# One packed constant table for three, loaded from ScalarE's queue together with the large tile's x

## The chip, the cores and the metric

The kernel runs on one core of a Trainium2 chip. The metric is device time in microseconds for one execution of the whole step; a time of a kernel is the median of its runs.

## What is computed

The reference is one inference step of one hybrid decoder layer: 2048 prompt tokens behind 16 learned meta tokens, and 8 decoding sequences of 4 tokens, all of width 1024. One projection feeds four token mixers of width 256, each mixer is gated, and the four go together through an output projection.

```python
h = rmsnorm(x, norm_pre)
c = split(h @ w_in)                       # 14 groups of 256 columns, and 16 for the low rank
log_a = log_sigmoid(c.a_lr @ gla_w_a2 + gla_b_a) / 16
o_a = gated_linear(c.a_q / 8, c.a_k, c.a_v, log_a, s_gla)      # 4 heads of 64
o_b = c.b_b * causal_conv3(c.b_c * c.b_v) * silu(c.b_z)
o_c = gated_linear(silu(c.c_q) / 8, 1 - f, c.c_i, log f, s_hgrn)
o_d = (trailing_means(c.d_v) - c.d_v) @ pool_w * pool_scale * silu(c.d_z)
x = x + rmsnorm(concat(o_a, o_b, o_c, o_d) @ w_out, norm_post)
```

The two gated linear mixers also get a head norm and a SiLU gate. `gla_w_a2` with its bias is the gate matrix (`a2` in the kernel), `pool_w` are the pool weights (`pw`), and the masks (`cu8`) are the byte masks that VectorE uses in the running sums (keep or restart) and in copying scores.

## The kernel before

The tokens are cut into a small tile 0 (16 meta tokens and the 32 sample tokens, T0 = 48) and eight large tiles of 256 tokens, each loaded in two chunks of 128 rows. So x(1, 0) and x(1, 1) are the two halves of the first large tile. Both halves go into the same buffer `xin`, so that x(1, 1) may be loaded only when the transposes of x(1, 0) have read it.

All engines run hand-written orders. Before the steady loop the kernel prepares its weights: `w_in` comes as 28 units of 512 KB (`unit`, L411 to L418), eight staging areas lie in the buffers `wo_hi` and `wo_lo` (units 0 to 3 and 4 to 7 of each round), and each unit is turned into an fp16 upper half on ScalarE (`upper`, L1245) and an fp16 rest on VectorE (`lower`, L1827). A unit from number 8 on is loaded when `lower` has freed its staging area. Matmuls are done as three fp16 products.

The start is ordered as follows.

- SyncE (L420 to L440) issues: meta and sample tokens (L373, L374), the table `cf32` (L421), the low-rank weights (L422), x(1, 0) (L382), units 0 and 1, the gate matrix `a2` of 97 rows (L426), the masks `cu8` (L427), units 2 and 3, the pool and convolution states, then x(1, 1) behind a wait for the transposes of x(1, 0), units 4 to 7, the two recurrent states, `pw` (L437), and units 8 to 27.
- ScalarE (L1536 on): table load, low-rank weights (L1539, which needs VectorE's L2204, and that needs `cf32` and the low-rank weights), norm of tile 0, norm of x(1, 0), upper half of tile 0's activations (L1292), `upper` 0 and 1, `upper` 2, the low-rank output of tile 0 (L1303), upper half of x(1, 0) (L1292), the logarithm for tile 0, `upper` 3, norm of x(1, 1) (L1267), `upper` 4 and 5, upper half of x(1, 1), and so on.
- TensorE: transposes of tile 0 and of x(1, 0) (L762), the low rank of tile 0 (L733), the gate product (L746, needs `a2`), transposes of x(1, 1), then projections (L695).
- VectorE: its part of the norms (L1842), the rest of the activations (L1858), `lower` 0 to 2, x(1, 0), the first running sum (L1880, needs `cu8`), `lower` 3, x(1, 1) (L1842, L1858), then `lower` 4 to 7 and on.

In the profile, `cu` is the mask table, `a` the gate matrix, `cf` the table `cf32`, `X<-in_w_lr` the low-rank weights.

Of the kernel before, what the change touches and what calls it, by code (L numbers as in the profile page):

```python
# [8 lines left out]
U8 = mybir.dt.uint8  # L9
# [5 lines left out]
GW = 256  # L15
NCF, NCU = 319, 1024
HK = 64
RANK = 16
LRG = 3
LRP = 2 * RANK * LRG  # L20
# [5 lines left out]
CH = 128  # L26
# [18 lines left out]
NSTAGE = 8  # L45
# [21 lines left out]
def fill_order():  # L67
# [29 lines left out]
    xin=32, xre=32, yst=32,  # L97
# [5 lines left out]
    gs=28, ge=14, gm=28, sc=32, am=32,  # L103
# [17 lines left out]
def nth(name, i, k):  # L121

    if name in ("tcp", "tlc"):
        return 1 if i == 0 else 2
    if name in ("xhi", "xlo", "hx"):
        return (i - TURNED) * SIGNALS[name] + k
    if i == 0:
        return k
    return (0 if name in OWN0 else FIRST.get(name, SIGNALS[name])) + (i - 1) * SIGNALS[name] + k


def dims(i):

    return (T0, 1, T0) if i == 0 else (TT, 2, CH)
# [18 lines left out]
def program(nc, a, outs):  # L153
    ctx = ExitStack()
    with ctx:
        def sb(name, shape, dt=F32):
            return ctx.enter_context(nc.sbuf_tensor(name, shape, dt))
# [13 lines left out]
        XIN = sb("xin", [128, D])  # L171
# [9 lines left out]
        X1, X3, X4 = (sb(f"X{n}", [128, 2, TT + 16]) for n in (1, 3, 4))  # L181
        X2 = sb("X2", [128, 2, TT])
        cf32 = sb("cf32", [128, NCF])
        cu8 = sb("cu8", [128, NCU], U8)
        pw = sb("pw", [128, 2, 128])
        a2 = sb("a2", [LRP + 1, GW])
        lrb = sb("lrb", [LRP + 1, TT])
        cst = sb("cst", [128, 2])
        sx = sb("sx", [128, 3])
# [7 lines left out]
        ident, bones, gs = cf32[:, 0:128], cf32[:, 128:256], cf32[:, 256:256 + KD]  # L197
# [15 lines left out]
        tin = X4[:, :, :].rearrange("p j t -> p (j t)")  # L213
# [81 lines left out]
        def keys_of(i, br, rows):  # L295
# [8 lines left out]
        s0 = {n: ctx.enter_context(nc.semaphore("f_" + n)) for n in OWN0}  # L304
        s["pj"] = ctx.enter_context(nc.semaphore("s_pj"))
        once = {n: ctx.enter_context(nc.semaphore("o_" + n)) for n in (
            "cf32", "cu8", "a2", "lrw", "tin", "pw", "smp", "zero", "cst", "gs", "wlr", "wlrh", "gp",
            "whi", "wlo", "wohi", "wolo", "ylast", "lsq", "xlast", "sdec", "vx", "su", "sv", "svout", "tl", "sout", "fin", "pd0",
            "act", "dve", "pool")}
        for n in range(NSTAGE):  # L310
# [6 lines left out]
        def sem(name, i):  # L317
            return (s0 if i == 0 and name in OWN0 else s)[name]

        def at(name, i, k):  # L320
            if i == 1 and k == 0 and name in OWN0:
                i, k = 0, FIRST.get(name, SIGNALS[name])
            return sem(name, i), nth(name, i, k)
# [21 lines left out]
        def bank(i, name):  # L345
            return pj[FILL[i, name] % 2]

        block = ctx.enter_context(nc.Block())
        dve, act, pool, pe = nc.vector, nc.scalar, nc.gpsimd, nc.tensor
# [20 lines left out]
        def _(sp):  # L370
            def load_x(i, c):
                if i == 0:
                    sp.dma_start(XRES[0:META, :], a["meta_tokens"]).then_inc(sem("xin", i), 16)  # L373
                    sp.dma_start(XRES[META:T0, :], a["x_sample"].rearrange("b t d -> (b t) d")).then_inc(sem("xin", i), 16)  # L374
                    return
                if c == 0 and i > 1:
                    sp.wait_ge(*(at("xt", i - 1, 4) if i <= TURNED else at("xlo", i - 1, 2)))
                elif c == 1:
                    sp.wait_ge(*(at("xt", i, 2) if i < TURNED else at("xlo", i, 1)))
                if c == 0 and i == 2:  # L380
                    sp.wait_ge(once["su"], 4)
                sp.dma_start(XIN[:, :], a["x_prompt"][(i - 1) * TT + c * CH:(i - 1) * TT + c * CH + CH, :]  # L382
                             ).then_inc(sem("xin", i), 16)
# [28 lines left out]
            def unit(u):  # L412

                if u >= NSTAGE:
                    sp.wait_ge(once["whi"], 2 * (u - NSTAGE + 1))
                    sp.wait_ge(once["wlo"], 2 * (u - NSTAGE + 1))
                sp.dma_start(stage[u % NSTAGE], a["w_units"][u].rearrange("p (k n) -> p k n", k=2)
                             ).then_inc(once["wld%d" % (u % NSTAGE)], 16)  # L418
# [1 line left out]
            load_x(0, 0)  # L420
            sp.dma_start(cf32[:, :], a["c_f32"]).then_inc(once["cf32"], 16)  # L421
            sp.dma_start(lr_stage, a["w_lr"].rearrange("p (k n) -> p k n", k=KD)).then_inc(once["lrw"], 16)  # L422
            load_x(1, 0)
            for u in range(0, 2):
                unit(u)
            sp.dma_start(a2[:, :], a["a2"]).then_inc(once["a2"], 16)  # L426
            sp.dma_start(cu8[:, :], a["c_u8"]).then_inc(once["cu8"], 16)  # L427
            for u in range(2, 4):
                unit(u)
            sp.dma_start(tin[0:DB * POOLB, 0:GW], a["state_pool"].rearrange("b t c -> (b t) c")).then_inc(once["tin"], 16)  # L430
            sp.dma_start(tin[0:DB * 2, GW:2 * GW], a["state_conv"].rearrange("b t c -> (b t) c")).then_inc(once["tin"], 16)
            load_x(1, 1)
            for u in range(4, NSTAGE):
                unit(u)
            for br, name in enumerate(("state_gla", "state_hgrn")):
                sp.dma_start(SS[br], a[name].rearrange("p (b j v) -> p b j v", b=DB, j=2)).then_inc(once["smp"], 16)
            sp.dma_start(pw[:, :, :], a["c_pw"]).then_inc(once["pw"], 16)  # L437
            for u in range(NSTAGE, NU):
                unit(u)
            sp.dma_start(outs["pool_sample"][:, 0:POOLB - DS, :], a["state_pool"][:, DS:POOLB, :]).then_inc(once["sout"], 16)  # L440
# [8 lines left out]
            for u in range(2 * KD):  # L449
                n, k, col = u % 4, u // 2, 512 * (u % 2)  # L450
# [223 lines left out]
        def fill_wait(i, name):  # L674

            n = FILL[i, name]
            if n >= 2:
                before = FILLS[n - 2]
                who, k = reader(*before)
                pe.wait_ge(*at(who, before[0], k))  # L680
# [56 lines left out]
        def log_alpha(i):  # L737
            T, NC, C = dims(i)
            b = bank(i, "la")
            fill_wait(i, "la")  # L740
            pe.wait_ge(*at("lr", i, 1))
            if i == 0:
                pe.wait_ge(once["a2"], 16)
                pe.wait_ge(once["zero"], 4)
            for j in range(2):
                m = pe.matmul(b[:, j * T:(j + 1) * T], a2[:, 128 * j:128 * j + 128], lrb[:, 0:T], start=True, stop=True)  # L746
            m.then_inc(s["pj"], 1)
# [129 lines left out]
        def pool_product(i):  # L877
            T, NC, C = dims(i)
            b = bank(i, "po")
            fill_wait(i, "po")  # L880
            pe.wait_ge(*at("pd", i, 1))
            if i == 0:
                pe.wait_ge(once["pw"], 16)
            for j in range(2):
                if i == 0:
                    pe.matmul(b[:, j * T:j * T + META], pw[:, j, :], X3[:, j, POOLB:POOLB + META], start=True, stop=True)
                    m = pe.matmul(b[:, j * T + META:j * T + T0].rearrange("p (b w) -> p b w", w=DS), pw[:, j, :],
                                  seqs(X3, 32, DB, POOLB + DS, POOLB, POOLB + DS)[:, j], start=True, stop=True)
                else:
                    m = pe.matmul(b[:, j * T:j * T + T], pw[:, j, :], X3[:, j, POOLB:POOLB + T], start=True, stop=True)  # L890
            m.then_inc(s["pj"], 1)
# [349 lines left out]
        def upper(u):  # L1241
            g, k = u // 4, 2 * (u % 4)
            act.wait_ge(once["wld%d" % (u % NSTAGE)], 16 * (u // NSTAGE + 1))
            for n in range(2):
                act.activation(w_hi[:, k + n, 2 * GW * g:2 * GW * (g + 1)], stage[u % NSTAGE][:, n, :], ACT.Copy,  # L1245
                               scale=gs[:, k + n:k + n + 1]).then_inc(*give1(act, "whi"))
# [33 lines left out]
        def x_hi(i, c):  # L1280
# [9 lines left out]
            for n in range(2):  # L1290
# [2 lines left out]
                               op[:, 512 * n:512 * n + 512].rearrange("p (k t) -> p k t", k=4)[:, :, 0:C],  # L1293
                               ACT.Copy).then_inc(*give(act, "hhi", i, 2 * c + n + 1))

        def low_rank_out(i):
            T, NC, C = dims(i)
            act.wait_ge(*filled(i, "lr"))
            if i == 0:
                act.wait_ge(once["zero"], 4)  # L1300
            elif i == 1:
                act.wait_ge(*filled(0, "la"))
            act.activation(lrb[0:LRP, 0:T], bank(i, "lr")[0:LRP, 0:T], ACT.Copy, scale=CS).then_inc(*give(act, "lr", i, 1))  # L1303
# [229 lines left out]

        @block.scalar
        def _(_act):
            act.preload_act_table_set("natural_log_exp_and_others")  # L1536
            act.wait_ge(once["cst"], 2)
            act.wait_ge(once["wlr"], 1)
# [3 lines left out]
            x_hi(0, 0)  # L1542
            upper(0)
            upper(1)
            upper(2)
            low_rank_out(0)
            x_hi(1, 0)
# [322 lines left out]
        def running_sum(i, br, t):  # L1870
            T, NC, C = dims(i)
            if i == 0:
                dve.wait_ge(once["cu8"], 16)
            elif i > 1:
                dve.wait_ge(*at("eq", i - 1, br + 1))
                dve.wait_ge(*at("dc", i - 1, br + 1))
                dve.wait_ge(*at("ks", i - 1, br + 1))
            dve.wait_ge(*own(dve))
            for j in range(2):
                m = dve.tensor_tensor_scan(b_of(i, br)[:, j, 0:T], (keep if i else keep0), t[:, j, 0:T], 0.0, ALU.mult, ALU.add)  # L1880
            m.then_inc(*give(dve, "bsc", i, br + 1))
# [691 lines left out]
```

## Time and profile before

| | us |
|---|---|
| median of 3 runs | 1046.09 |
| lowest and highest run | 1043.64, 1046.59 |
| the profiled execution's own time | 1043.29 |
| its span in the profile | 1041.3 |
| TensorE busy in the span | 991.8 (95%) |
| VectorE busy | 632.6 (61%) |
| ScalarE busy | 434.6 (42%) |

The span runs from the first to the last instruction; 2.0 us of the profiled execution lie around it. Times inside the trace are counted from the span's start. A row of the timeline gives start, duration, engine, line, operation, output and inputs, how many instructions were merged, and in brackets the idle time before and what ended it. Where several instructions are merged, the duration is that of the stretch from the first start to the last end.

### The profile page before, as it was taken

What the parts mean: (1) busy time and instruction counts of PE and PEld (TensorE: products, weight loads), DVE (VectorE), ACT (ScalarE), POOL (GpSimd) and SP (SyncE); (2) the same over time, 40 slices, a digit from 0 to 9 for tenths busy, and PEclk for the clock granted to TensorE, in tenths of its full rate; (3) what the DMA queues carried; (4) which work ended last, traced back from release to release, by engine and by line L of the source; (5) the groups of instructions that cost most, each with busy time, mean ns of one, the idle gap of its engine ahead of it and who ended that gap; (6) DMA issues with size and microseconds to landing.
All of it is one profiled execution on the core that took longest, in us unless ns stands there. A gap on an engine that the chain in (4) does not pass through costs nothing.

```text
span 1041.3 us, 27274 instructions
## 1 busy us (share of the span) xinstructions
PE 991.8 (95%) x11684; PEld 736.7 (71%) x11684; DVE 632.6 (61%) x1333; ACT 434.6 (42%) x849; POOL 383.4 (37%) x526
## 2 busy tenths in 40 slices
PE   2998799999999999999999999999999999999997
PEld 2867577855886668865887668865877668866783
DVE  4997679645845567445745567445735467346564
ACT  6874454532533334431534334432534325243333
POOL 1534441174305550174305550174304651256300
PEclk9997799999999999999999999999999999999999
DMA  8730331001220013001220012101220012100011
GB/s 320 263 104 4 128 127 55 14 2 42 62 62 1 3 61 66 37 2 42 63 62 2 1 63 62 42 2 42 62 62 1 2 63 52 31 2 25 18 66 43
DMA packets 41530, 56.23 MB, mean 54 GB/s; under 512 B 27793, under 2 KB 28603, under 8 KB 41403
## 3 DMA queue, kind: packets, MB, share of 16 engines
q1 hardware_dynamic: 41411, 54.51, 16.7%
q8 instruction: 92, 1.51, 0.6%
q14 instruction: 27, 0.22, 0.1%
HBM read 38.44 MB, written 9.86 MB: 46 GB/s over the span
## 4 chain that ended last, share of the span: by engine, by line
PE 66%; DVE 20%; ACT 8%; issue 3%; DMA 1%; SPq 1%; POOL 0%; DVEq 0%; ACTq 0%
PE pj L695 29%; PE op L918 15%; PE pj L714 7%; PE sc L793 5%; DVE A L1945 3%; DVE w_lo L1827 3%; DVE X L2139 1%; ACT xres L1267 1%; ACT xres L1278 1%; DVE X L2146 1%; PE sc L938 1%; PE op L938 1%; DVE A L1957 1%; PE m L898 1%; PE m L850 1%
## 5 line engine op out<-in xcount | busy, mean ns | idle before, releaser
L695 PE MATMUL pj<-h_hi,w_hi 128*128 128x256 f16 (+1 forms) x1728 | 210.6, 265 | 0.6
L695 PE MATMUL pj<-h_lo,w_hi 128*128 128x256 f16 (+1 forms) x1728 | 209.2, 264 | 0.0
L695 PE MATMUL pj<-h_hi,w_lo 128*128 128x256 f16 (+1 forms) x1728 | 208.6, 264 | 0.0
L1945 DVE COPY_PREDICATED A<-cu,sc 64x128 f32<-64x128 uint8 x384 | 132.0, 344 | 113.7 <-PE sc L793 107.2
L520 POOL TENSOR_TENSOR G<-B 128x256 f32<-128x256 f32 x112 | 79.0, 706 | 286.9 <-DVE B L1880 163.9
L695 PEld LDWEIGHTS pj<-h_hi,w_hi 128*128 128x128 f16 x1728 | 151.2, 99 | 28.1 <-issue 4.4
L695 PEld LDWEIGHTS pj<-h_lo,w_hi 128*128 128x128 f16 x1728 | 158.2, 99 | 17.7
L695 PEld LDWEIGHTS pj<-h_hi,w_lo 128*128 128x128 f16 x1728 | 157.7, 98 | 17.4
L531 POOL TENSOR_TENSOR G<-G,Q 128x256 f32<-128x256 f32 x112 | 86.6, 773 | 114.8 <-issue 46.8
L1367 ACT ACTIVATE G<-G 128x512 f32<-128x512 f32 x112 | 69.1, 621 | 77.4 <-POOL G L521 77.3
L532 POOL TENSOR_TENSOR G<-G,K 128x256 f32<-128x256 f32 x112 | 92.6, 827 | 0.0
L793 PEld LDWEIGHTS sc<-G 64*64 64x64 f32 x3072 | 55.6, 137 | 33.9 <-issue 25.7
L521 POOL TENSOR_TENSOR G<-B 128x256 f32<-128x256 f32 x112 | 77.2, 689 | 0.0
L793 PE MATMUL sc<-G 64*64 64x32 f32 x3072 | 66.1, 224 | 4.6 <-DVE A L1945 4.0
L1226 ACT ACTIVATE X<-pj 128x512 f32<-128x512 f32 (+1 forms) x45 | 24.7, 548 | 85.3 <-PE pj L695 66.8
L2133 DVE SCALAR_TENSOR_TENSOR X<-X 128x512 f32<-128x512 f32 x32 | 24.5, 766 | 55.6 <-ACT X L1226 53.4
L918 PE MATMUL op<-wo_hi,m_hi 128*128 128x512 f16 x224 | 53.2, 380 | 0.0
L918 PE MATMUL op<-wo_lo,m_hi 128*128 128x512 f16 x224 | 52.9, 379 | 0.0
L918 PE MATMUL op<-wo_hi,m_lo 128*128 128x512 f16 x224 | 52.9, 379 | 0.0
L1957 DVE COPY_PREDICATED A<-cu,sc 64x256 f32<-64x256 uint8 x64 | 28.4, 444 | 28.0 <-PE sc L804 26.9
L1939 DVE COPY A<-sc 64x128 f32<-64x128 f32 x64 | 18.4, 287 | 37.9 <-PE sc L781 34.5
L918 PEld LDWEIGHTS op<-wo_lo,m_hi 128*128 128x128 f16 x224 | 21.9, 98 | 26.4
(289 smaller groups left out, 1366.2 us busy)
## 6 DMA issues: line engine op xcount, KB each, us to landing
xin<-in_x_prompt SPq DMA_DIRECT2D x17, 512.0 KB, 4.0
wo_hi<-in_w_units SPq DMA_DIRECT2D x16, 512.0 KB, 5.3
xres<-in_x_prompt SPq DMA_DIRECT2D x15, 512.0 KB, 3.6
out_y_prompt<-xres SPq DMA_DIRECT2D x14, 512.0 KB, 2.6
wo_lo<-in_w_units SPq DMA_DIRECT2D x12, 512.0 KB, 6.3
xres<-in_w_out SPq DMA_DIRECT2D x8, 256.0 KB, 2.9
gpost<-in_w_out SPq DMA_DIRECT2D x8, 256.0 KB, 4.2
m_hi<-in_state_gla SPq DMA_DIRECT2D x1, 512.0 KB, 8.4
```

Of the source, the lines that this page charges most:

```text
L520: pool.tensor_tensor(Gv[R], Bv[R], mid, ALU.subtract).then_inc(*give(pool, "gs", i, 2 * n + 1))
L521: pool.tensor_tensor(Gv[L], mid, Bv[L], ALU.subtract).then_inc(*give(pool, "gs", i, 2 * n + 2))
L531: pool.tensor_tensor(Gv[R], Gv[R], Qv[R], ALU.mult).then_inc(*give(pool, "gm", i, 2 * n + 1))
L532: pool.tensor_tensor(Gv[L], Gv[L], Kv[L], ALU.mult).then_inc(*give(pool, "gm", i, 2 * n + 2))
L695: m = pe.matmul(b[:, j * T:(j + 1) * T], w[:, k, col + 128 * j:col + 128 * j + 128], h[:, k, :], start=(n == 0 and k == 0), stop=(n == 2 a ...
L714: m = pe.matmul(b[0:C, :], h[:, k, c * CH:c * CH + C], w[:, k, col:col + 2 * GW], start=(n == 0), stop=(n == 23))
L793: m = pe.matmul(out, L, R, start=True, stop=True)
L918: m = pe.matmul(op[0:C, 512 * n:512 * n + 512], x[:, k, c * CH:c * CH + C], w[:, k, 512 * n:512 * n + 512], start=(p == 0 and k == 0), sto ...
L1367: act.activation(g, g, ACT.Exp, scale=SCALE[br]).then_inc(*give(act, "ge", i, n + 1))
L1827: dve.scalar_tensor_tensor(w_lo[:, k + n, col], stage[u % NSTAGE][:, n, :], gs[:, k + n:k + n + 1], w_hi[:, k + n, col], ALU.mult, ALU.sub ...
L1945: m = dve.copy_predicated(out, mk.unsqueeze(1).broadcast_to([64, 4, 32 // h, h]), half(SC[hh], u)[:, 0:128].rearrange("p (q b w) -> p q b ...
L1957: m = dve.copy_predicated(half(A[hh], u)[:, :, 64 * u:64 * u + 64], mk, half(SC[hh], u)[:, 0:256].rearrange("p (q t) -> p q t", t=64))
```

## The change

The three tables `cu8`, `pw` and `a2` become parts of one SBUF tensor `mix` of 128 rows by 3 KB, packed on the host and loaded with one transfer from ScalarE's queue. ScalarE's queue also loads both halves of the first large tile: x(1, 0) as its first instruction, x(1, 1) between `upper` 1 and `upper` 2, behind a wait for the transposes of x(1, 0). SyncE's queue keeps the rest and issues units 0 to 7 one behind another, directly after the low-rank weights. The waits on the three tables become waits on the one.

```diff
-        cu8 = sb("cu8", [128, NCU], U8)
-        pw = sb("pw", [128, 2, 128])
-        a2 = sb("a2", [LRP + 1, GW])
+        mix = sb("mix", [128, 3 * GW])
+        cu8 = mix[:, 0:GW].bitcast(U8)
+        pw = mix[:, GW:2 * GW].rearrange("p (j n) -> p j n", j=2)
+        a2 = mix[0:LRP + 1, 2 * GW:3 * GW]
...
             sp.dma_start(lr_stage, a["w_lr"].rearrange("p (k n) -> p k n", k=KD)).then_inc(once["lrw"], 16)
-            load_x(1, 0)
-            for u in range(0, 2):
-                unit(u)
-            sp.dma_start(a2[:, :], a["a2"]).then_inc(once["a2"], 16)
-            sp.dma_start(cu8[:, :], a["c_u8"]).then_inc(once["cu8"], 16)
-            for u in range(2, 4):
+            for u in range(0, NSTAGE):
                 unit(u)
...
-            load_x(1, 1)
-            for u in range(4, NSTAGE):
-                unit(u)
...
-            sp.dma_start(pw[:, :, :], a["c_pw"]).then_inc(once["pw"], 16)
...
-                pe.wait_ge(once["a2"], 16)
+                pe.wait_ge(once["mix"], 16)
...
-                pe.wait_ge(once["pw"], 16)
+                pe.wait_ge(once["mix"], 16)
...
+        def load_first(c):
+            if c:
+                act.wait_ge(*at("xt", 1, 2))
+            act.dma_start(XIN[:, :], a["x_prompt"][c * CH:c * CH + CH, :]).then_inc(sem("xin", 1), 16)
+
...
         def _(_act):
+            load_first(0)
+            act.dma_start(mix[:, :], a["c_mix"]).then_inc(once["mix"], 16)
             act.preload_act_table_set("natural_log_exp_and_others")
...
             upper(1)
+            load_first(1)
             upper(2)
...
-                dve.wait_ge(once["cu8"], 16)
+                dve.wait_ge(once["mix"], 16)
```

## Rows read from the trace of the kernel before

**Rows 1.** The page, first part: busy time, share of span, instructions.

```profile
PE 991.8 (95%) x11684; PEld 736.7 (71%) x11684; DVE 632.6 (61%) x1333; ACT 434.6 (42%) x849; POOL 383.4 (37%) x526
```

**Rows 2.** The chain that ended last, 0 to 62 us: start, duration, what.

```profile
4.40 3.14 SPq L427
7.58 8.21 DMA wo_hi<-in_w_units
...
34.70 2.91 DVE w_lo L1827 x4
```

**Rows 3.** The timeline of SyncE's DMA issues, 2 to 12.5 us.

```profile
2.12 0.43 SPq L422 DMA_DIRECT2D X<-in_w_lr  x1
2.59 0.43 SPq L382 DMA_DIRECT2D xin<-in_x_prompt  x1
...
4.02 0.33 SPq L426 DMA_DIRECT2D a<-in_a  x1
4.40 3.14 SPq L427 DMA_DIRECT2D cu<-in_c_u  x1
...
12.06 0.35 SPq L382 DMA_DIRECT2D xin<-in_x_prompt  x1
```

**Rows 4.** DMA issues by size and us to landing, windows around single issues.

```profile
xres<-in_meta_tokens SPq DMA_DIRECT2D x1, 64.0 KB, 2.1
...
cf<-in_c_f SPq DMA_DIRECT2D x1, 159.5 KB, 2.3
...
X<-in_w_lr SPq DMA_DIRECT2D x1, 64.0 KB, 2.0
...
xin<-in_x_prompt SPq DMA_DIRECT2D x1, 512.0 KB, 4.3
...
cu<-in_c_u SPq DMA_DIRECT2D x1, 128.0 KB, 10.1
...
xin<-in_x_prompt SPq DMA_DIRECT2D x1, 512.0 KB, 6.7
```

**Rows 5.** Stretches of 2 us: the last two columns are DMA share and GB/s.

```profile
2.00:4.00 2.00, 0.00 (x0) 0.00 (x0) 0.00 (x0) 0.03 (x1) 0.28 (x1) 1.00 0.83 194
...
8.00:10.00 2.00, 0.77 (x8) 0.61 (x6) 1.28 (x3) 1.93 (x7) 0.00 (x0) 1.00 0.78 197
...
12.00:14.00 2.00, 0.38 (x17) 0.25 (x16) 1.13 (x2) 0.00 (x0) 0.00 (x0) 1.00 0.87 249
...
16.00:18.00 2.00, 0.71 (x4) 0.71 (x4) 0.82 (x2) 2.00 (x5) 0.00 (x0) 1.00 1.03 412
```

**Rows 6.** The timeline of ScalarE, 0 to 21 us.

```profile
0.75 1.28 ACT L1536 ACT_TABLE_LOAD   x1 [0.75 <-PEq L2528]
4.68 0.31 ACT L1539 ACTIVATE w_lr<-X 128x128 f16<-128x128 f32 x1 [2.65 <-DVE X L2204]
...
9.04 2.55 ACT L1245 ACTIVATE w_hi<-wo_hi,cf 128x512 f16<-128x512 f32 x4
15.81 1.33 ACT L1245 ACTIVATE w_hi<-wo_hi,cf 128x512 f16<-128x512 f32 x2 [4.23 <-DMA wo_hi<-in_w_units]
...
20.61 1.06 ACT L1267 ACTIVATE X<-xin 128x1024 bf16<-128x1024 f32 x1
```

**Rows 7.** The timeline of TensorE and VectorE, first and last step of x's path.

```profile
10.09 1.94 PE L762 MATMUL op<-cf,xin 128*128 128x128 f32 x8 [1.31 <-DVE h_lo L1858]
...
25.29 1.29 DVE L1858 TENSOR_TENSOR h_lo<-op,h_hi 128x512 f16<-128x512 f32 x2 [2.17 <-ACT h_hi L1292]
```

**Rows 8.** Stretches: length, busy of PE, PEld, DVE, ACT, POOL, granted clock.

```profile
40.00:60.00 20.00, 19.31 (x232) 13.44 (x230) 19.65 (x49) 17.50 (x39) 7.30 (x10) 1.00 0.83 281
...
81.50:88.30 6.80, 6.80 (x114) 6.35 (x114) 4.36 (x19) 4.97 (x17) 1.91 (x3) 0.50 0.01 2
...
98.60:109.00 10.40, 6.07 (x102) 3.60 (x99) 9.51 (x36) 4.18 (x13) 5.62 (x9) 0.50 0.01 3
109.00:119.10 10.10, 7.35 (x97) 5.28 (x95) 4.17 (x9) 4.44 (x15) 3.94 (x7) 0.50 0.23 60
```

More of the change, by code:

```diff
@@ L306, in program @@
         once = {n: ctx.enter_context(nc.semaphore("o_" + n)) for n in (
-            "cf32", "cu8", "a2", "lrw", "tin", "pw", "smp", "zero", "cst", "gs", "wlr", "wlrh", "gp",
+            "cf32", "mix", "lrw", "tin", "smp", "zero", "cst", "gs", "wlr", "wlrh", "gp",
             "whi", "wlo", "wohi", "wolo", "ylast", "lsq", "xlast", "sdec", "vx", "su", "sv", "svout", "tl", "sout", "fin", "pd0",
@@ L375, in load_x @@
                     return
-                if c == 0 and i > 1:
+                if c == 0:
                     sp.wait_ge(*(at("xt", i - 1, 4) if i <= TURNED else at("xlo", i - 1, 2)))
-                elif c == 1:
+                else:
                     sp.wait_ge(*(at("xt", i, 2) if i < TURNED else at("xlo", i, 1)))
@@ L2559 @@
     add("c_f32", f32)
-    add("c_u8", u8)
     pw = np.zeros((128, 2, 128), np.float32)
@@ L2563 @@
         pw[64 * (g % 2):64 * (g % 2) + 64, g // 2, 64 * (g % 2):64 * (g % 2) + 64] = w
-    add("c_pw", pw)
     rank = np.asarray(inputs["gla_w_a2"])[0]
-    add("a2", np.ascontiguousarray(np.concatenate([rank] * (2 * LRG) + [np.asarray(inputs["gla_b_a"])])))
+    mix = np.zeros((128, 3 * GW), np.float32)
+    mix[:, 0:GW] = u8.view(np.float32)
+    mix[:, GW:2 * GW] = pw.reshape(128, -1)
+    mix[0:LRP + 1, 2 * GW:] = np.concatenate([rank] * (2 * LRG) + [np.asarray(inputs["gla_b_a"])])
+    add("c_mix", mix)
     outs = {name: nc.dram_tensor("out_" + name, shape, F32, kind="ExternalOutput").ap() for name, shape, _ in _OUTS}
```

## The prediction

> **What bounds the kernel now.** I read the page's busy shares first. TensorE is busy for 95% of the span [rows 1], so a change that adds or removes no arithmetic can only win in the time when TensorE isn't yet fed. All that this change touches lies in the first 27 us. So the second view is the chain of work that ended last, cut to the first 62 us, and what to look for is where it runs through a transfer and not through an engine. It does so once: SyncE stands 3.14 us in issuing the masks, and behind that the third weight unit (unit 2) takes 8.21 us, from 7.58 to 15.79 [rows 2]. From 34.70 on the chain is mostly VectorE making the weights' rests [rows 2], and VectorE is busy for 19.65 of the 20 us from 40 to 60 [rows 8].
>
> The third view is ScalarE's timeline, to see who wants that unit. ScalarE ends `upper` 1 at 9.04 + 2.55 = 11.59 and starts `upper` 2 at 15.81, with 4.23 us of idle time ended by the transfer [rows 6]. What stands behind `upper` 2 on ScalarE is the low-rank output of tile 0, the upper half of x(1, 0), `upper` 3 and the norm of x(1, 1) at 20.61, and ScalarE works on that row nearly without a gap. VectorE's last real wait at the start is for the upper half of x(1, 1), 2.17 us, and it starts that subtraction at 25.29 [rows 7]; after it VectorE has work without end. So whatever brings `upper` 2 forward brings 25.29 forward by the same amount, as VectorE does the same instructions before it, and all that follows waits on engines and not on a clock on the wall.
>
> **Why unit 2 is late.** SyncE issues `a2` at 4.02 in 0.33 us and `cu8` at 4.40 in 3.14 us, where its neighbours take 0.43 [rows 3]. The 128 KB of `cu8` land 10.1 us after their issue, at 14.5, while x(1, 0), four times as large, took 4.3 [rows 4]. The DMA engines meanwhile don't run at their rate: 197 GB/s from 8 to 10 us and 249 from 12 to 14, against 412 from 16 to 18 [rows 5]. In these two stretches (412 - 197 + 412 - 249) x 2 us = 0.76 MB weren't moved, which is 1.8 us at 412 GB/s. A few engines with long queues and the others without work fit these rows. The Trainium skill ("DMA: Bandwidth & Descriptors", "Why a DMA increments its semaphore by 16 and not by 1") says that a transfer uses the largest number of engines up to 16 that divides its row count, so that the 97 rows of `a2` would all go to one. By that rule the trace agrees: the masks and unit 2 wait on that one engine. The sum below needs only that units 0 to 7 and the packed table have 128 rows each, like x(1, 0).
>
> **The change, part by part.**
>
> *SyncE's queue.* It loses x(1, 0), `a2` and `cu8` ahead of unit 2: 0.43 + 0.33 + 3.14 = 3.9 us of issue and 0.15 of gaps. Unit 2 would be issued near 3.6 and not at 7.58. Ahead of its end are 64 + 128 + 160 + 64 KB of small loads, 512 of x, 384 of the packed table and 1536 of units 0 to 2, in all 2.92 MB. At 412 GB/s from about 2 us that is 9.1. If the stretch 2 to 4 us stays at 194 GB/s [rows 5], then 0.39 MB are moved by 4, and 2.53 MB more at 412 end at 10.1; with a receipt of up to 1 us, 11.1. All are before ScalarE can want it (12.5 below), so this wait is gone, and the question is what is late next.
>
> *ScalarE's queue, the first two issues.* None was issued from ScalarE before. SyncE's rows give 0.35 to 0.43 each when nothing stands in the way; zero and 3.14 are the ends. I take 0.43: two make 0.9 us ahead of the table load of 1.28 us, which then ends near 3.0 and not at 2.03. ScalarE waited 2.65 us before its first activation at 4.68 [rows 6], so this costs nothing; at 3.14 for one of them the table load would end at 5.7 and cost 1 us. I take nothing.
>
> *The small loads that ScalarE's first activation needs.* This is the cost of the change. Now `cf32` and the low-rank weights land at 3.95 and 4.12 (2.3 and 2.0 us after their issue) [rows 3, 4], scarcely more than the 2.1 of the meta tokens, the shortest, and nothing large is ahead of them. After the change 512 KB of x and 384 KB of the table are issued beside them from 0.75 on. The ends: the small loads pass freely, 0 us; all 0.92 MB go ahead, 0.92 / 0.412 = 2.2 us. At the rate of the 2 to 4 us stretch, 194 GB/s, it would be 4.7. Two queues that take turns give the middle of the first two, and I take 1.1 us. The chain from there is gapless: low-rank weights, norm of tile 0, norm of x(1, 0) (whose load, earlier now, gives back 0.1), `upper` 0 and 1, and on TensorE the transposes of x(1, 0), which end at 10.09 + 1.94 = 12.03 [rows 7]. They move to 13.0.
>
> The Trainium skill (same page, "Queues, rings and completion order" and "Issuing engines are not separate DMA queues") says that both queues run on the same 16 engines, which take turns between them. It speaks against this change: a second issuing engine adds no bandwidth, and the small loads get half of it. By it the 1.1 stands; with both queues free of each other the sum would be 1.1 better. No row of before shows two queues at work.
>
> *ScalarE's third issue.* x(1, 1) is issued between `upper` 1 and `upper` 2, behind a wait for the transposes. ScalarE ends `upper` 1 at 11.59 + 1.0 = 12.6, then waits for the transposes to 13.0, issues for 0.43 + 0.04, and starts `upper` 2 at 13.5. The wait and the issue hold up `upper` 2, whose unit is there, by 0.9 us, and with it the low-rank output of tile 0 and TensorE's gate product. So `upper` 2 starts 15.81 - 13.5 = **2.3 us** earlier.
>
> *x(1, 1) itself.* Issued at 13.0, not 12.06 [rows 3], wanted at 20.61 - 2.3 = 18.3. So it has 5.3 us. The first x took 4.3 behind four small loads and the second 6.7 behind units on a queue that was held up [rows 4]. Worked out: the meta tokens' 2.1 for 64 KB, 448 KB more at 412 GB/s for 1.1, and as much again for the other queue's turns, 1.3, make 4.5. It lands at 17.5, in time by 0.8.
>
> *The rest.* `pw` goes from SyncE (0.45 us where nobody waits). The gate product, the running sum and the pool product wait for the packed table, which lands by about 6, long before the first of them. Units 3 to 7 are issued some us earlier, and are never late. Units from 8 on wait for `lower`, so they move with VectorE. The masks are the same bytes for VectorE. I cost these at nothing; their cover is that no engine waits for a transfer between 16 and 62 us.
>
> The sum: 2.3 us off. Against the profiled execution's own time that is 1043.29 - 2.3 = 1041.0. That execution lies 2.8 us below the median of the runs, so on the median it is 1046.09 - 2.3 = **1043.8**. The ends of the forecast's own terms are 3.4 (small loads free) and 1.2 (all of x and the table ahead).
>
> **The rivals.**
>
> *Free small loads.* The two queues don't disturb the first 4 us, since the engines run at only 194 GB/s from 2 to 4 [rows 5]. Then the transposes end at 12.0, `upper` 2 starts at 12.45 and the gain is 3.4: 1042.7.
>
> *x(1, 1) becomes the wait.* If the second half queues behind all that SyncE has issued by 13.0 (units 6, 7, two states of 512 KB each and small ones), its latency is the 6.7 of before or more. Then it lands at 19.7 or later against 18.3 and the gain falls to 0.9: 1045.2. For it: the deep queue. Against it: it stands on another ring.
>
> *The start gets slower within the noise.* The small loads lose 4.7 us, at 194 GB/s. It decides from 3.4 us on, and gives 1.3 us more: 1047.4.
>
> *TensorE's clock, for us.* From 81.5 to 88.3 and from 98.6 to 119.1 the granted clock is 0.50, that is 1.2 GHz and not 2.4. In the first it is busy for all 6.80 us [rows 8]. If the earlier start spares that one, up to half is won, 3.4, so 5.7 in all: 1040.4.
>
> *TensorE's clock, against us: slower.* The same mechanism, the other way. If the shifted start brings about one more stretch like that from 98.6 to 119.1, with 6.07 + 7.35 = 13.4 us busy [rows 8], the work costs 6.7 us more. Against a gain of 2.3 it is +4.4: 1050.5. It decides from a busy half-clock stretch of 4.6 us on, where 2.3 are lost. For it: two such stretches exist. Against it: everything after 27 us keeps its order and its relative times.
>
> *The change doesn't do what it says:* unit 2 stays late, as other transfers are in its way, and nothing changes: 1046.1.
>
> **How the numbers follow.** Forecast 0.42; free small loads 0.15; clock for us 0.14; x(1, 1) late 0.12; slower start 0.06; clock against us 0.08; no effect 0.03. The bound of 0.3%, about what a measurement of this kernel can tell from no change, is 3.1 us. Faster by more: the free small loads, the clock for us and the upper edge of the forecast, 0.15 + 0.14 + 0.04 = 0.33. Slower by more: the clock against us, 0.08. Within: 0.59. The range is 1040.0 to 1047.5: it leaves out the clock against us and about half of the clock for us. The forecast's own range is 1042.7 to 1044.9.
>
> **What would show it.** Right: ScalarE starts `upper` 2 near 13.5 behind a wait for TensorE and not for a DMA; the low-rank weights land near 5.2; VectorE's subtraction for x(1, 1) starts near 23.0; no stretch from 6 to 16 us falls below about 350 GB/s. Wrong: `upper` 2 ends a wait for a unit; the norm of x(1, 1) waits for `xin`; a gain at 23 us that is lost by 130 us, where another chain would have taken over; half-clock stretches of another length.

## The result and the profile after

The changed kernel takes 1048.38 us against 1046.01 us for the kernel before, a ratio of 1.0022 with a 95% interval of 1.0012 to 1.0031. It is 0.2% slower, by 2.4 us, where 2.3 us of gain were forecast. The profiled execution took 1048.53 us, its span is 1046.4. One run of 3509.57 us is left out of the comparison as disturbed.

The first reading is the page's first row, against [rows 1]: the same instructions, the same shares.

```profile
PE 995.7 (95%) x11684; PEld 739.6 (71%) x11684; DVE 634.0 (61%) x1333; ACT 434.9 (42%) x849; POOL 383.9 (37%) x526
```

The second is the timeline of ScalarE and of its queue (`ACTq`) in the changed kernel, against [rows 6].

```profile
0.74 0.42 ACTq L1291 DMA_DIRECT2D xin<-in_x_prompt  x1
1.19 0.46 ACTq L1534 DMA_DIRECT2D mix<-in_c_mix  x1
1.68 1.28 ACT L1535 ACT_TABLE_LOAD   x1 [1.68 <-PEq L2528]
7.86 0.31 ACT L1538 ACTIVATE w_lr<-X 128x128 f16<-128x128 f32 x1 [4.89 <-DVE X L2204]
...
12.21 2.55 ACT L1237 ACTIVATE w_hi<-wo_hi,cf 128x512 f16<-128x512 f32 x4
15.21 0.33 ACTq L1291 DMA_DIRECT2D xin<-in_x_prompt  x1
15.59 1.33 ACT L1237 ACTIVATE w_hi<-wo_hi,cf 128x512 f16<-128x512 f32 x2 [0.83 <-PE op L754]
...
22.56 1.06 ACT L1259 ACTIVATE X<-xin 128x1024 bf16<-128x1024 f32 x1 [2.26 <-DMA xin<-in_x_prompt]
```

The wait for unit 2 is gone, as forecast. `upper` 2 (the row at 15.59) now ends a wait for TensorE's transposes. But everything ahead of it is 3.2 us late, from the first activation on (7.86, and 4.68 before), so that `upper` 2 starts only 0.2 us earlier. Then the norm of x(1, 1) meets a wait that wasn't there, 2.26 us, and starts at 22.56 and not at 20.61.

The third view, the DMA issues with their us to landing, says which loads those were, against [rows 4].

```profile
xres<-in_meta_tokens SPq DMA_DIRECT2D x1, 64.0 KB, 3.1
...
cf<-in_c_f SPq DMA_DIRECT2D x1, 159.5 KB, 5.5
...
X<-in_w_lr SPq DMA_DIRECT2D x1, 64.0 KB, 5.3
...
xin<-in_x_prompt ACTq DMA_DIRECT2D x1, 512.0 KB, 4.7
...
mix<-in_c_mix ACTq DMA_DIRECT2D x1, 384.0 KB, 5.5
...
xin<-in_x_prompt ACTq DMA_DIRECT2D x1, 512.0 KB, 7.3
```

`cf32` takes 5.5 us and not 2.3, the low-rank weights 5.3 and not 2.0, and x(1, 1), the last row, 7.3. The queues from 1 to 6 us say what went ahead of the two small loads (q10 is ScalarE's queue, q1 SyncE's; packets, MB, share of the 16 engines).

```profile
q10 hardware_dynamic: 278, 0.91, 57.5%
q1 hardware_dynamic: 138, 0.25, 25.3%
```

By 6 us ScalarE's queue has moved 0.91 of its 0.92 MB, and SyncE's little more than the 0.20 MB of tokens that stand ahead of `cf32`. VectorE's timeline has the step that all later work hangs on, against [rows 7]: it starts 1.94 us later than before.

```profile
27.23 1.29 DVE L1858 TENSOR_TENSOR h_lo<-op,h_hi 128x512 f16<-128x512 f32 x2 [2.17 <-ACT h_hi L1284]
```

Once the start is over, the DMA engines did better, as was expected without the 97-row load: where they ran at 197 and 249 GB/s [rows 5], they now move 410 (last column). Before that, with both queues starting, it was 263 and 290.

```profile
2.00:4.00 2.00, 0.00 (x0) 0.00 (x0) 0.00 (x0) 0.96 (x1) 0.28 (x1) 1.00 0.73 263
4.00:6.00 2.00, 0.00 (x0) 0.00 (x0) 0.00 (x0) 0.00 (x0) 0.00 (x0) 1.00 1.03 290
...
8.00:10.00 2.00, 0.00 (x0) 0.00 (x0) 0.29 (x1) 1.81 (x5) 0.00 (x0) 1.00 1.03 410
...
12.00:14.00 2.00, 0.77 (x4) 0.80 (x5) 1.51 (x4) 2.00 (x4) 0.00 (x0) 1.00 1.03 410
```

So more bytes were moved earlier, and the wrong ones first.

### The profile page after: what moved, and what is told of

Same layout as the page of the kernel before. It is cut to its first block, busy times and chain, and to the rows that moved or that the text cites. A ratio compares the mean times of both kernels' runs of the same rounds, so it can differ in the third digit from the quotient of the medians.

```text
span 1046.4 us, 27272 instructions
## 1 busy us (share of the span) xinstructions
PE 995.7 (95%) x11684; PEld 739.6 (71%) x11684; DVE 634.0 (61%) x1333; ACT 434.9 (42%) x849; POOL 383.9 (37%) x526
## 3 DMA queue, kind: packets, MB, share of 16 engines
q10 hardware_dynamic: 432, 1.44, 0.4%
## 4 chain that ended last, share of the span: by engine, by line
PE 67%; DVE 20%; ACT 8%; issue 3%; DMA 2%; DVEq 0%; SPq 0%; ACTq 0%
PE pj L687 30%; PE op L910 15%; PE pj L706 7%; PE sc L785 5%; DVE A L1945 3%; DVE w_lo L1827 3%; DVE X L2139 1%; PE m L890 1%; ACT xres L1259 1%; ACT xres L1270 1%; DVE X L2146 1%; PE sc L930 1%; PE op L930 1%; DVE A L1957 1%; PE m L827 1%
## 5 line engine op out<-in xcount | busy, mean ns | idle before, releaser
L1945 DVE COPY_PREDICATED A<-mix,sc 64x128 f32<-64x128 uint8 x384 | 132.0, 344 | 113.0 <-PE sc L785 106.6
L1957 DVE COPY_PREDICATED A<-mix,sc 64x256 f32<-64x256 uint8 x64 | 28.5, 445 | 28.4 <-PE sc L796 27.3
```

Of the source, the lines that this page charges most:

```text
L1945: m = dve.copy_predicated(out, mk.unsqueeze(1).broadcast_to([64, 4, 32 // h, h]), half(SC[hh], u)[:, 0:128].rearrange("p (q b w) -> p q b ...
L1957: m = dve.copy_predicated(half(A[hh], u)[:, :, 64 * u:64 * u + 64], mk, half(SC[hh], u)[:, 0:256].rearrange("p (q t) -> p q t", t=64))
```

## The experiments

**The two parts apart.** The first run packs the tables and leaves every load on SyncE. A second kernel, after a repeat of the first, doesn't even pack: it only pads the gate matrix. The diffs in this section show the lines that matter, and the plus lines are the run's.

```diff
+            sp.dma_start(mix[:, :], a["c_mix"]).then_inc(once["mix"], 16)
-            sp.dma_start(a2[:, :], a["a2"]).then_inc(once["a2"], 16)
-            sp.dma_start(cu8[:, :], a["c_u8"]).then_inc(once["cu8"], 16)
...
-            sp.dma_start(pw[:, :, :], a["c_pw"]).then_inc(once["pw"], 16)
```

> One part alone: the three tables packed into one of 128 rows, but issued by SyncE in the place of a2 and cu8, with everything else in the order of before. Theory (the packing removes the hold, the loads on ScalarE's queue cost more than it gives): unit 2 lands near 10.5 us, upper 2 starts near 11.7 directly after upper 1, the low-rank weights land near 4.1 as before, x(1, 1) lands near 16.5; VectorE's subtraction for x(1, 1) starts near 21.3 (25.29 before), and the time is some 4 us under before, 1042. Rival (the packing brings nothing, the wait for unit 2 comes from the transfers' total bytes): upper 2 near 15.8 and a time within 1 us of before.

Measured: 1041.48 us, ratio 0.9959 of the time before (95% interval 0.9942 to 0.9975). The subtraction for x(1, 1) starts at 21.49 us. ScalarE goes from `upper` 1 to `upper` 2 with 0.19 us of idle time. The unit's landing is the wait, but a short one:

```profile
12.01 1.33 ACT L1244 ACTIVATE w_hi<-wo_hi,cf 128x512 f16<-128x512 f32 x2 [0.19 <-DMA wo_hi<-in_w_units]
...
21.49 1.29 DVE L1857 TENSOR_TENSOR h_lo<-op,h_hi 128x512 f16<-128x512 f32 x2 [2.17 <-ACT h_hi L1291]
```

The run was repeated for its interval, with no further edit.

> The kernel with the packed table on SyncE once more, for its interval: 0.994 to 0.998 of the time before, VectorE's subtraction near 21.5.

Measured: 1042.39 us, ratio 0.9959 (0.9942 to 0.9977), the subtraction at 21.37.

Now the kernel before with the gate matrix padded to 128 rows.

```diff
-        a2 = sb("a2", [LRP + 1, GW])
+        a2 = sb("a2", [128, GW])
...
-    add("a2", np.ascontiguousarray(np.concatenate([rank] * (2 * LRG) + [np.asarray(inputs["gla_b_a"])])))
+    a2 = np.zeros((128, GW), np.float32)
+    a2[0:LRP + 1] = np.concatenate([rank] * (2 * LRG) + [np.asarray(inputs["gla_b_a"])])
+    add("a2", a2)
```

> The kernel before with one edit: the gate matrix is loaded as 128 rows (31 of them zeros) and not 97; the masks and the pool weights stay transfers of their own. Theory (97 rows all go to one DMA engine, which then is behind the others): the masks' issue takes 0.4 us and not 3.14, they land under 6 us after issue and not 10.1, and upper 2 starts before 12 us; the time is as in the run with the packed table on SyncE, some 4 us under before. Rival (it is the small rows of the masks, or the number of transfers, that hold the queue): the masks' issue stays near 3 us and upper 2 near 15.8.

Measured: 1042.97 us, ratio 0.9962 (0.9948 to 0.9976), the subtraction at 21.37. The masks, still a transfer of their own with rows of 1 KB, are issued in 0.80 us and not 3.14 (0.4 was expected). They land after 6.1 and not 10.1; under 6 was expected. ScalarE runs `upper` 0, 1 and 2 as one group:

```profile
4.49 0.80 SPq L427 DMA_DIRECT2D cu<-in_c_u  x1
...
cu<-in_c_u SPq DMA_DIRECT2D x1, 128.0 KB, 6.1
...
9.45 3.78 ACT L1245 ACTIVATE w_hi<-wo_hi,cf 128x512 f16<-128x512 f32 x6
```

So, within the intervals, the whole gain of packing is that of 31 more rows in one small table. It needed no change to the masks and no fewer transfers. The kept traces also record each increment of a load's semaphore, and these show where the wait comes from:

| semaphore increments recorded, us | 97 rows (before) | 128 rows |
|---|---|---|
| gate matrix | 2: at 4.47 and 14.18 | 16: from 8.93 to 10.23 |
| masks | 15 by 10.88, the last at 14.51 | 16: from 9.28 to 10.59 |
| unit 2 | 14 by 12.36, then 14.71 and 15.79 | 16: from 10.56 to 11.87 |

The gate matrix of 97 rows has one increment 0.1 us after its issue has ended and one more 9.7 us later, and of the masks behind it all but one sixteenth is there 3.6 us before the rest. That is how one late engine with all 97 rows looks; the trace doesn't number the engines, and why unit 2 has a second late one stays open. It is the rule of the Trainium skill ("DMA: Bandwidth & Descriptors", "Why a DMA increments its semaphore by 16 and not by 1"), with which both runs agree.

**Why the small loads are late.** One run on the changed kernel puts them first on ScalarE's queue, another leaves only x(1, 0) and no table on it at the start.

```diff
         def _(_act):
+            act.dma_start(cf32[:, :], a["c_f32"]).then_inc(once["cf32"], 16)
+            act.dma_start(lr_stage, a["w_lr"].rearrange("p (k n) -> p k n", k=KD)).then_inc(once["lrw"], 16)
             load_first(0)
```

> The changed kernel with cf32 and the low-rank weights issued first on ScalarE's queue, ahead of x(1, 0) and the packed table, and no longer on SyncE's. Theory (the two small loads were late because x and the table on the other queue went ahead of them): cf32 lands near 4 us and not 7.16, ScalarE's first activation starts near 4.7 and not 7.86, the transposes end near 12.1, upper 2 starts near 12.6; x(1, 1), issued near 12.1 beside SyncE's long backlog, still takes about 7.3 us and lands near 19.4, which the norm of x(1, 1) waits for, so VectorE's subtraction starts near 24.1: 1 us under before, 3 under the changed kernel. Rival (the DMA engines start late with two queues, whichever load is first): cf32 still lands after 6 us.

Measured: 1048.13 us, ratio 1.0016 (1.0004 to 1.0029). The start of the theory holds, its end doesn't. `cf32` lands after 3.0 us, and the first activation starts at 4.83. But now x(1, 0), third on that queue, takes 7.1 us and costs ScalarE 1.82, while SyncE's units go ahead; x(1, 1) takes 8.1 and costs 3.06.

```profile
xin<-in_x_prompt ACTq DMA_DIRECT2D x1, 512.0 KB, 7.1
...
cf<-in_c_f ACTq DMA_DIRECT2D x1, 159.5 KB, 3.0
...
8.76 1.06 ACT L1257 ACTIVATE X<-xin 128x1024 bf16<-128x1024 f32 x1 [1.82 <-DMA xin<-in_x_prompt]
22.05 1.06 ACT L1257 ACTIVATE X<-xin 128x1024 bf16<-128x1024 f32 x1 [3.06 <-DMA xin<-in_x_prompt]
```

So here the harm goes to the large load behind the others, x(1, 0), and no longer to the small ones. The subtraction is at 26.72 and not at the 24.1 expected, because the expectation left out this wait of 1.8 us and took 7.3 us for x(1, 1), not 8.1.

```diff
-            act.dma_start(mix[:, :], a["c_mix"]).then_inc(once["mix"], 16)
...
-            for u in range(0, NSTAGE):
+            for u in range(0, 2):
+                unit(u)
+            sp.dma_start(mix[:, :], a["c_mix"]).then_inc(once["mix"], 16)
+            for u in range(2, NSTAGE):
                 unit(u)
```

> The changed kernel with the packed table issued by SyncE behind unit 1 and not by ScalarE; both halves of x stay on ScalarE's queue. Theory (what is queued on ScalarE's queue goes ahead of cf32 in proportion to its descriptors): x(1, 0) alone, 8 of the 16 rows per engine, delays cf32 by half of the 3.2 us, so it lands near 5.5 and not 7.16 and ScalarE's first activation starts near 6.2; x(1, 1), issued near 13.6 beside the same backlog, still waits over 7 us and lands near 21.2, and VectorE's subtraction starts near 25.9. The time is near before's, 1046 to 1047. Rival (only the table hurts): cf32 lands at 4 and the subtraction starts before 25.

Measured: 1047.69 us, ratio 1.0008 (0.9995 to 1.002). `cf32` lands 4.6 us after its issue, at 6.3, which is 2.3 us late (1.5 expected), against 3.2 us in the changed kernel with both large loads. So x(1, 0) alone does most of the harm. x(1, 1) took 7.2 us, and the subtraction starts at 26.17 (25.9 expected).

**Why x(1, 1) is late.** The first run here thins SyncE's backlog (what it has issued and the DMA engines haven't moved yet). The two after it build that backlog into the kernel with the packed table on SyncE, with x(1, 1) on the second queue and on the same one.

```diff
-            for u in range(0, NSTAGE):
+            for u in range(0, 4):
                 unit(u)
...
+            sp.wait_ge(*at("xt", 1, 2))
+            for u in range(4, NSTAGE):
+                unit(u)
             for br, name in enumerate(("state_gla", "state_hgrn")):
```

> The changed kernel with SyncE waiting for the transposes of x(1, 0) before units 4 to 7 and the recurrent states, so that little is queued when ScalarE issues x(1, 1). Theory (x(1, 1) took 7.33 us because its descriptors got their turn only behind what SyncE had queued): it takes about 5 us, the norm of x(1, 1) doesn't wait for it (2.26 us of wait in the changed kernel), and VectorE's subtraction starts near 25.0 and not 27.23, with the late start of the small loads left as it is. Rival (7.3 us is what a second queue costs): the wait stays at about 2 us and the subtraction at 27.

Measured: 1045.98 us, ratio 1.0002 (0.999 to 1.0015). x(1, 1) takes 5.0 us and ScalarE doesn't wait for it; the subtraction starts at 24.88. With this one wait gone, the change is worth nothing, because the 3 us at the start are left. The edit also makes units 4 to 7 later, and the run can't say what that alone costs.

```profile
xin<-in_x_prompt ACTq DMA_DIRECT2D x1, 512.0 KB, 5.0
...
24.88 1.29 DVE L1861 TENSOR_TENSOR h_lo<-op,h_hi 128x512 f16<-128x512 f32 x2 [2.18 <-ACT h_hi L1287]
```

The next run keeps the packed table on SyncE and moves only x(1, 1) to ScalarE's queue, so that units 4 to 7 and the states are issued ahead of it and don't wait for the transposes.

```diff
             upper(1)
+            load_second()          # waits for the transposes, issues x(1, 1)
             upper(2)
...
-            load_x(1, 1)
             for u in range(4, NSTAGE):
                 unit(u)
```

> The best kernel so far (the packed table on SyncE, 1041.48 us) with x(1, 1) on ScalarE's queue and units 4 to 7 issued ahead of it by SyncE, so that the backlog stands as in the changed kernel but nothing disturbs the first 4 us. Theory: x(1, 1) is issued near 12.3, takes 7 us or more and lands near 19.5, where ScalarE wants it at 17.2; the subtraction starts near 24.2 and not 21.49, and the time is 2 to 3 us over that kernel, 1044. Rival (x(1, 1) was late in the changed kernel only because all was late): it lands by 17 and the time stays at 1041.5 to 1042.

Measured: 1045.4 us, ratio 0.9989 (0.998 to 0.9998). x(1, 1) takes 7.0 us and costs ScalarE 1.88, plus 0.89 ahead of `upper` 2, which holds the wait for the transposes and the issue of 0.38. The subtraction starts at 23.75, and 3 of the 4 us that the packing brings are gone.

The last one of these has the same backlog, but x(1, 1) is issued by SyncE, behind it.

```diff
-            load_x(1, 1)
             for u in range(4, NSTAGE):
                 unit(u)
             for br, name in enumerate(("state_gla", "state_hgrn")):
                 ...
+            load_x(1, 1)
```

> The kernel with the packed table on SyncE, and x(1, 1) issued by SyncE too, but behind units 4 to 7 and the two recurrent states: the backlog of the run with x(1, 1) on ScalarE's queue (where it took 7.0 us from issue to landing and 1.88 us of ScalarE's time), on one queue instead of two. Theory A (the second queue gets a turn only when what the DMA engines already hold has been moved, and shares after that): in one queue x(1, 1) waits for the whole backlog and lands later, near 12.3 + 8 = 20.3; ScalarE waits near 3 us, the subtraction starts near 25 and the time is over that run's 1045.4. Theory B (the second queue brings no turn at all under a backlog): landing after 7 us, ScalarE waits 1.9 us, 1045.4.

Measured: 1048.76 us, ratio 1.0025 (1.0011 to 1.0039). x(1, 1) takes 10.3 us (8 expected) and costs ScalarE 5.93 (3 expected); the subtraction starts at 27.24 (25 expected).

```profile
xin<-in_x_prompt SPq DMA_DIRECT2D x1, 512.0 KB, 10.3
...
22.57 1.06 ACT L1266 ACTIVATE X<-xin 128x1024 bf16<-128x1024 f32 x1 [5.93 <-DMA xin<-in_x_prompt]
```

So theory B is out, and theory A has the direction and too small a size: with the same backlog ahead a queue of its own saves x(1, 1) 3.3 us, 7.0 against 10.3. It doesn't bring it to the front. How late the turn comes is to be seen in the changed kernel's DMA queues. x(1, 1) was issued at 15.21 on ScalarE's queue, q10. The first two rows are from 15.3 to 19.3 us, the last two from 19.3 to 23.

```profile
q1 hardware_dynamic: 529, 1.44, 104.2%
q10 hardware_dynamic: 2, 0.01, 0.5%
...
q1 hardware_dynamic: 274, 1.00, 67.4%
q10 hardware_dynamic: 142, 0.52, 35.1%
```

For four microseconds next to nothing of x is moved, while SyncE's queue moves 1.44 MB. Then the queues share. Not all of the four is the backlog's: in the run with the short backlog, where the engines stood idle when x(1, 1) was issued at 14.99, its first packet starts between 16.3 and 16.4. So about 1.3 us pass even then, and the backlog adds about 2.7. The other kernels with the backlog and two queues agree: from issue to the first packet of x(1, 1) it is 3.5 us with the small loads first, 3.8 with x(1, 1) alone on ScalarE and 3.9 with the table on SyncE. The Trainium skill ("DMA: Bandwidth & Descriptors", "Queues, rings and completion order") has the engines take turns between the queues. The second pair of rows agrees with that, and the first pair doesn't: turns begin some 2.7 us later than they could. That the engines already hold this much work from the first queue would explain both pairs; no run shows what they hold.

**A good use of the second queue?** In the kernel with the packed table on SyncE, ScalarE's queue now takes only the two small loads.

```diff
-            sp.dma_start(cf32[:, :], a["c_f32"]).then_inc(once["cf32"], 16)
-            sp.dma_start(lr_stage, a["w_lr"].rearrange("p (k n) -> p k n", k=KD)).then_inc(once["lrw"], 16)
...
+            act.dma_start(cf32[:, :], a["c_f32"]).then_inc(once["cf32"], 16)
+            act.dma_start(lr_stage, a["w_lr"].rearrange("p (k n) -> p k n", k=KD)).then_inc(once["lrw"], 16)
             act.preload_act_table_set("natural_log_exp_and_others")
```

> The same best kernel with cf32 and the low-rank weights issued from ScalarE's queue, idle at that time, so that SyncE issues x(1, 0) 0.9 us earlier; the large loads all stay on one queue. Theory (small loads on the second queue go ahead, large ones there do the harm): cf32 lands near 3.7, x(1, 0) near 6.2, the first activation starts near 4.7 and the norm of x(1, 0) near 6.8; the subtraction starts near 21.1 and the time is 0.3 to 0.5 us under that kernel, near 1041.1. Rival: as two queues disturb each other anyway, x(1, 0) lands after 7.1 as in the run with the small loads first, 8.7, and the time is 1 us or more over.

Measured: 1042.56 us (1041.1 expected), ratio 0.9958 (0.9945 to 0.997), not to be told from the packing on SyncE alone. `cf32` is a little earlier (VectorE's first use at 3.48), but x(1, 0), issued 0.93 us earlier, took 5.5 us and landed at 7.1 as ever. The subtraction is at 21.36. The gain in the issue is given back in the landing.

**Is it the late start, and only that?** This run delays the kernel before and changes nothing else.

```diff
+            for _ in range(2 if (i, c) == (1, 1) else 0):
+                act.activation(junk[0:C, :], xin_of(i)[0:C, :], ACT.Square).then_inc(*give1(act, "act"))
+                act.wait_ge(*own(act))
```

> The kernel before with a known delay and nothing else: two more squarings of x(1, 1) on ScalarE (results thrown away) ahead of its norm, about 1 us each, where the changed kernel waits for that load. VectorE's subtraction for x(1, 1) should start near 27.2 and not 25.29, as in the changed kernel (27.23). Theory (the changed kernel's loss is that delay, and TensorE's clock adds to it on the way): the median is 1.6 to 3 us over before, as the changed kernel's 2.4, with the granted clock half for longer than before's 27.3 us in the profile. Rival (something else in the changed kernel costs time later, the packed table's place or the second queue): this run is only 1.6 to 1.9 us over before and its half-clock stretches are those of before.

Measured: 1048.06 us, ratio 1.0016 (1.0004 to 1.0028). In its profile unit 2 happened to land 0.75 us earlier than before, so the subtraction started at 26.71, 1.4 us late, and not at the 27.2 expected. The ratio is a loss of 1.7 us, which lies in the range of the theory and in that of its rival, so the time doesn't decide between them. Nor do the stretches at a granted clock of 0.5, some 31 us against 27 before: two profiles of the kernel with the packed table on SyncE have 34 and 27. The run with x(1, 1) behind the backlog is the better witness: with one queue only, its subtraction starts at 27.24, as the changed kernel's at 27.23, and the ratios are 1.0025 and 1.0022. So nothing speaks for a further cost of the second queue later on. Ordered by this one time of the profiled executions, the kernels fall in line, but for the one with the short backlog, whose ratio can't be told from 1:

| kernel | subtraction for x(1, 1) starts, us | ratio |
|---|---|---|
| small loads on ScalarE, packed on SyncE | 21.36 | 0.9958 |
| gate matrix of 128 rows | 21.37 | 0.9962 |
| packed on SyncE (twice) | 21.49, 21.37 | 0.9959, 0.9959 |
| x(1, 1) alone on ScalarE | 23.75 | 0.9989 |
| changed kernel, short backlog | 24.88 | 1.0002 |
| before | 25.29 | 1 |
| changed kernel, table on SyncE | 26.17 | 1.0008 |
| before, delayed | 26.71 | 1.0016 |
| changed kernel, small loads first | 26.72 | 1.0016 |
| changed kernel | 27.23 | 1.0022 |
| packed, x(1, 1) behind the backlog | 27.24 | 1.0025 |

From first to last it is 5.9 us in the subtraction and 0.0067 x 1046 = 7.0 us in the time. The 1.1 us between them is no more than the intervals, 1.3 and 1.5 us to either side, allow.

## Why the prediction was wrong, point by point

1. *What bounds the start.* Right. The chain ran through unit 2, and the subtraction for x(1, 1) carries what the start wins or loses to the end, as the table shows.
2. *Why unit 2 is late.* Right, and shown by the padded gate matrix. The gain of 3.9 us at the subtraction is more than the 3.4 that the prediction gave as the upper end, since ScalarE without the third issue doesn't wait for the transposes either. (It started `upper` 2 directly behind `upper` 1, near 11.9.)
3. *The small loads, taken as 1.1 us between 0 and 2.2.* **Here the sum failed first.** It was 3.2 us (7.86 - 4.68). The middle assumed that the queues take turns from the start; in fact nearly all of ScalarE's 0.92 MB went ahead (0.91 by 6 us). And the upper end, 0.92 MB at 412 GB/s, assumed engines already at full rate. They moved 263 GB/s from 2 to 4 us and 290 from 4 to 6, and 0.92 MB at their mean of 276 would be 3.3 us, which fits the 3.2. Even the 64 KB of the meta tokens, first in their queue, took 3.1 us and not 2.1. Why two queues start at these rates no run shows. The slow end, 4.7 at 194 GB/s, was computed, and kept for a rival with a chance of 0.06.
4. *ScalarE's third issue.* Right in size, 0.9 us forecast: ScalarE stood for 0.83 us between `upper` 1 and `upper` 2, some 0.45 until the transposes ended and then an issue of 0.33. `upper` 2 started at 15.59 and not at 13.5, because the transposes ended at 15.2.
5. *x(1, 1) itself, taken as 4.5 us.* **Here the sum failed again.** It took 7.3. Issued at 15.2, it had 5.1 us until ScalarE stood ready at 20.3 (22.56 less the wait of 2.26), about the 5.3 that the prediction gave it. The term let x(1, 1) move at once, after a start of 2.1 us, and gave the other queue only as many bytes. In the trace its first bytes come 4 us after the issue, behind 1.44 MB of the other queue, and turns only after that. The prediction had this as a rival with 6.7 us, and held against it that the load stands on another ring; that other ring saved 3.3 us and not the wait.
6. *The rest at nothing.* Right; no other new wait stands in the profile.
7. *The rivals.* Two of them came true at once, the slower start (3.2 us of its 4.7) and the late x(1, 1). They were priced apart, and their chances were set as though one excluded the other. Both come from large loads on a second queue, one disturbing and one being disturbed, so together they deserved one case: 15.81 - 15.59 = 0.2 us won at `upper` 2, 2.26 lost ahead of the norm, which starts 22.56 - 20.61 = 1.95 later than before. It ends on the slower side, and the prediction's range, up to 1047.5, didn't reach it.
8. *TensorE's clock.* It explains the single profile and not the median. The two profiled spans differ by 5.1 us, of which 1.9 are in the subtraction. Over the 54 us from 81 to 135, the granted clock (third column from the right) was 0.65 in the changed kernel and 0.75 before, where 1 is 2.4 GHz:

```profile
81.00:135.00 54.00, 43.80 (x779) 35.24 (x778) 37.58 (x117) 25.34 (x75) 24.35 (x33) 0.65 0.20 61
...
81.00:135.00 54.00, 43.17 (x796) 35.13 (x793) 39.92 (x117) 26.61 (x77) 24.28 (x33) 0.75 0.22 71
```

But the kernel with the table on SyncE has it both ways, with its subtraction at 21.49 and at 21.37, and spans of 1040.7 and 1037.3:

```profile
76.00:130.00 54.00, 43.75 (x777) 34.83 (x778) 37.17 (x115) 25.34 (x75) 24.33 (x33) 0.68 0.20 65
...
76.00:130.00 54.00, 43.23 (x806) 35.06 (x806) 39.74 (x121) 26.82 (x78) 24.29 (x33) 0.75 0.23 71
```

This is scatter of one and the same kernel, 3.4 us wide. In the medians it doesn't show: the granted clock over the whole span has a median of 0.984 in the changed kernel's runs and of 0.984 in the 27 of the kernel before that stand beside the first experiment. Of the 2.4 us between the medians, 1.9 are in the subtraction, and the 0.5 that is left is less than the interval of 1.3 to 3.2 us can resolve. So neither rival of the clock is borne out.

## What to carry to other kernels

When a stall is traced to a transfer, look first at the row count of the small transfers queued ahead of it: padding 97 rows to 128 was worth 0.4% here, alone. In this kernel a load on a second queue didn't get ahead of what was already queued, and large loads issued there first went ahead of the small urgent loads on the other. So check both before you move a load: how much the first queue holds by then, and which urgent loads are issued just after. And before pricing two rivals apart, ask if one mechanism brings both.

## What the runs showed of the hardware that wasn't expected

- A load on an idle second queue beside a backlog had to wait: 7.0 to 8.1 us from issue to landing for 512 KB, of which 3.5 to 4.0 us passed before its first packet (1.3 with the engines idle), against 3.5 us on a single queue with little ahead and 10.3 behind the backlog on one queue.
- Two queues starting together with a large load on the second cost more than their bytes: the first 64 KB took 3.0 to 3.1 us, and 2.1 to 2.4 when the second queue's first load was small or there was none.
- One load of 97 rows left two semaphore increments in the trace where 128 rows left sixteen, and of the masks and units 2 and 3 behind it one or two sixteenths landed 2 to 4 us after the rest.
- An issue can itself be held up: the masks took 3.14 us to issue behind the 97 rows, 2.50 in another profile of the same start, and 0.80 behind 128 rows. What holds it no run shows.
